# Recurrent heads of a gated linear recurrence: score outputs issued ahead of the chain of states, and a head's closing norm moved into the next head's step

## The chip, the cores and the metric

One core of one Trainium2 chip runs the whole program. The metric is the device time of one execution in microseconds (us); lower is better.

## What is computed

The program is three stacked blocks. The change touches one layer of the second, a gated linear recurrence with 16 heads of 128 key and 128 value features, run forwards and backwards over 512 tokens, each direction started from a state that 256 context tokens leave. Cut to what matters:

```python
def _chunk_gla(q, k, v, g, s0):                      # per head, chunks of tokens
    def step(state, inp):
        bcum = jnp.cumsum(gc, axis=-2)
        b_ref, b_end = bcum[..., mid:mid + 1, :], bcum[..., -1:, :]
        inter = jnp.einsum('bhck,bhkv->bhcv', qc * jnp.exp(bcum), state)
        scores = jnp.einsum('bhtk,bhsk->bhts', qc * jnp.exp(bcum - b_ref), kc * jnp.exp(b_ref - bcum))
        intra = jnp.einsum('bhts,bhsv->bhtv', jnp.where(mask, scores, 0.0), vc)
        new_state = (jnp.exp(b_end[..., 0, :])[..., None] * state
                     + jnp.einsum('bhsk,bhsv->bhkv', kc * jnp.exp(b_end - bcum), vc))
        return new_state, inter + intra

def _hgrn_readout(o, gate, norm_g, w_out):           # o = forwards + backwards
    o = _rmsnorm(o, norm_g)
    o = o.reshape(o.shape[0], o.shape[1], E_WIDTH).astype(gate.dtype)
    return (o * jax.nn.silu(gate)) @ w_out
```

## The kernel before

The function `hgrn` does the 16 heads. Its work is written out by hand as one instruction stream per engine, and `steps` calls the same `step(h, p, par, r)` on every engine: a step projects head `h` (the next one) and does the recurrence of head `p = h - 1`. Step 0 has only a projection, the last step only a recurrence, and the steps between are a loop of two steps a turn. Waits between engines are counts of marks (`PR` of TensorE, `AR` of ScalarE, `DR` of VectorE, `GM` of GpSimd).

On TensorE a step is, in this order: the projections `kf`, the context's `kf`, `kb` (`project`, line 2402: 24 matmuls each of 512 or 256 columns); the recurrence of the forward direction, `recur(p, 0)`; the projections of the context's `kb`, `g` and `q`; `recur(p, 1)` for the backward direction; and the closing sum (line 2488). `recur` has four score products `sc0` to `sc3` (line 2427), transposes of the context's and the tokens' keys (2443, 2446), the context's state (2458), the four chunks' own states (2462), and then the outputs. VectorE meanwhile masks the scores (`copy_predicated`, line 2665, marks `m0`, `m1`: `sc2` reuses the PSUM bank of `sc0` and waits for `m0`, `sc3` waits for `m1`), and makes the four states that enter the chunks one from the other (2668 and three times 2673, marks `s0`, `ch0`, `ch1`, `st`). The outputs wait for the last of them:

```python
                on(pe, DR, p, f"st{d}")
                for i in range(TT):
                    o = K.ps[:, 6, i * P:(i + 1) * P]
                    pe.matmul(o, v[:, i, :], SC[:, d, i, :], ...)
                    mm = pe.matmul(o, S[:, i, :], QI[:, i * P:(i + 1) * P], ...)
```

So of the eight products of a direction, the four of line 2468 (values times scores) and the four of line 2470 (state times queries) alternate.

After the backward direction ScalarE squares the head's output (`sq`, 2588), TensorE sums the squares over the features (`sum`, 2488), ScalarE takes logarithm and exponential (`ln`, `rstd`, 2591 and 2593), and VectorE scales and gates the output (2743, 2746). TensorE's next step starts behind the sum; `sc0` of the next head waits for `ln`, since it writes the bank of the sum.

VectorE, after the states of the backward direction, does for the next head: scans of the keys' decays (2678, 2689), `arguments` (2630 to 2638), `lower` of the weights of `kb` (2621), then the output of the head before (2743, 2746), and in the next step `other_signs` (2702, 2678, 2689), 2644, the gate (2650), `dq0` and `qi0` (`factors`, 2652, 2654), `lower` of `g` (2621) and the first mask. GpSimd's three products a direction (2612) start behind the gate.

## Time and profile before

| | us |
|---|---|
| median of 3 runs | 4802.61 (4802.16 to 4806.18) |
| the profiled execution, its own time | 4801.64 |
| its span | 4799.9 |
| first to last projection matmul of `hgrn` (line 2402) | 1869.0 to 2599.9 |
| one step of the loop, from sum to sum | 47.5 |
| TensorE, VectorE, ScalarE, GpSimd busy in it | 43.96, 33.52, 28.78, 7.10 |

A row of the timeline gives the start, the duration, the engine and line, what it writes and reads with its shape, how many instructions are merged in it, and in brackets how long the engine sat idle before and who ended that. A 128x128 product of fp32 operands shows as two matmuls. The span is 1.7 us shorter than the execution's own time, and that is 1.0 us under the median.

### The profile page before, as it was taken

How to read it: one execution, taken by the hardware profiler on the slowest of the kernel's cores; microseconds unless marked ns; L12 is line 12 of the kernel's file. 1: busy time of each engine (PE TensorE's matmuls, PEld its weight loads, DVE VectorE, ACT ScalarE, POOL GpSimd, SP SyncE). 2: the span in 40 equal slices, each digit the busy share in tenths (PEclk: the TensorE clock that was granted, in tenths of full speed). 3: DMA queues.
4: the chain of work that ended last, by engine and by line, in shares of the span. 5: the costliest groups of instructions: out<-in, count | busy, mean ns of one | idle time of the engine just before them, and what ended most of it. 6: DMA issues, size and time to landing. Idle time of an engine off the chain costs nothing. (4 is left out here: it accounts for less than half of the span.)

```text
span 4799.9 us, 79096 instructions
## 1 busy us (share of the span) xinstructions
PE 4404.9 (92%) x32172; PEld 3339.1 (70%) x32172; DVE 2461.7 (51%) x3963; ACT 1610.6 (34%) x2467; POOL 334.4 (7%) x307
## 2 busy tenths in 40 slices
PE   8898999999999989999998899978998999899987
PEld 7665787775788767888887644456877567666675
DVE  3634543433535333676766379954534355455553
ACT  2324321323322233656565210143222233333332
POOL 0120000000000000111111000000000022211220
PEclk9889999999999999999999999989998999999998
DMA  3201222221122232111110312211222210000101
GB/s 144 107 19 70 88 105 92 88 88 53 71 105 88 108 124 83 47 58 50 54 54 34 125 68 81 77 53 72 104 97 81 93 37 20 20 20 20 55 3 53
DMA packets 36638, 337.15 MB, mean 70 GB/s; under 512 B 4080, under 2 KB 6384, under 8 KB 18544
## 3 DMA queue, kind: packets, MB, share of 16 engines
q1 hardware_dynamic: 36336, 332.76, 18.7%
q8 instruction: 234, 3.83, 0.3%
q14 instruction: 68, 0.56, 0.0%
HBM read 320.16 MB, written 12.58 MB: 69 GB/s over the span
## 5 line engine op out<-in xcount | busy, mean ns | idle before, releaser
L539 PE MATMUL ps<-hi,weight_parts 128*128 128x512 f32 x5136 | 1608.6, 394 | 121.7 <-DVE lo L406 76.7
L539 PEld LDWEIGHTS ps<-hi,weight_parts 128*128 128x128 f32 x5136 | 978.1, 190 | 341.3 <-issue 123.0
L539 PE MATMUL ps<-lo,weight_parts 128*128 128x512 f32 x2568 | 1010.4, 393 | 0.0
L527 DVE TENSOR_TENSOR weight_parts<-w,weight_parts 128x1024 fp32r<-128x1024 f32 (+1 forms) x336 | 407.0, 1213 | 966.9 <-ACT weight_parts L518 966.8
L518 ACT ACTIVATE weight_parts<-w 128x1024 fp32r<-128x1024 f32 (+1 forms) x336 | 351.7, 1048 | 1199.3 <-PE ps L539 996.0
L539 PEld LDWEIGHTS ps<-lo,weight_parts 128*128 128x128 f32 x2568 | 489.4, 191 | 101.9
L3500 PEld LDWEIGHTS ps<-buffers 64*64 64x64 f32 x12544 | 431.6, 136 | 143.0 <-issue 141.3
L3500 PE MATMUL ps<-buffers 64*64 64x64 f32 x12544 | 461.2, 226 | 69.9 <-issue 43.8
L2402 PE MATMUL ps<-x_parts,column_parts 128*128 128x512 f32 x1536 | 364.9, 395 | 9.9 <-DVE column_parts L2621 9.9
L2402 PEld LDWEIGHTS ps<-x_parts,column_parts 128*128 128x128 f32 x1536 | 287.7, 189 | 75.2 <-DVE column_parts L2621 10.4
L2857 PE MATMUL ps<-x,w 128*128 128x512 f32 x768 | 332.3, 596 | 6.8 <-PEq L815 6.8
L2920 DVE SCALAR_TENSOR_TENSOR buffers<-buffers,vecs 128x392 f32<-128x392 f32 (+14 forms) x480 | 286.8, 685 | 0.0
L2857 PEld LDWEIGHTS ps<-x,w 128*128 128x128 f32 x768 | 146.8, 191 | 191.5 <-issue 191.5
L3493 PE MATMUL ps<-h,w 128*128 128x512 f32 x512 | 228.4, 600 | 1.2 <-PEq L3324 1.2
L3493 PEld LDWEIGHTS ps<-h,w 128*128 128x128 f32 x512 | 96.2, 191 | 117.1 <-issue 115.6
L2427 PE MATMUL ps<-h 128*128 128x128 f32 x1024 | 128.3, 279 | 13.4 <-DVE h L2652 13.1
L2427 PEld LDWEIGHTS ps<-h 128*128 128x128 f32 x1024 | 124.9, 196 | 17.0 <-DVE h L2652 14.2
L3756 ACT ACTIVATE buffers<-ps 128x256 f32<-128x256 f32 x160 | 61.5, 385 | 202.2 <-PE ps L3500 196.2
L2621 DVE TENSOR_TENSOR column_parts<-w,column_parts 128x1024 fp32r<-128x1024 f32 x64 | 86.2, 1349 | 80.2 <-ACT column_parts L2501 80.2
L3481 POOL TENSOR_TENSOR buffers<-buffers,const 128x512 f32<-128x512 f32 x80 | 101.6, 1270 | 290.3 <-PE ps L3500 219.8
L2601 POOL MEMSET w<- 128x1024 f32 x1 | 1.0, 951 | 1539.7 <-POOLq L2130 1539.7
L785 PE MATMUL ps<-weight_parts,hi 128*128 128x512 f32 x320 | 100.3, 395 | 0.0
(481 smaller groups left out, 5394.4 us busy)
## 6 DMA issues: line engine op xcount, KB each, us to landing
w<-in_weights SPq DMA_DIRECT2D x126, 2048.0 KB, 7.6
w<-in_wh SPq DMA_DIRECT2D x64, 512.0 KB, 3.6
v_kept<-buffers SPq DMA_DIRECT2D x4, 1024.0 KB, 5.2
buffers<-v_kept SPq DMA_DIRECT2D x16, 256.0 KB, 2.6
h<-x_kept SPq DMA_DIRECT2D x2, 2048.0 KB, 10.5
x<-in_xT SPq DMA_DIRECT2D x4, 512.0 KB, 10.8
x_kept<-h SPq DMA_DIRECT2D x1, 2048.0 KB, 7.2
vc_kept<-x SPq DMA_DIRECT2D x4, 512.0 KB, 2.6
```

The lines of the kernel that those rows point to most:

```text
L518: act.activation(K.parts[:, j % 2, 0, 0:nk, :], part_of(K, slot, j, nk, by_row), ACT.Copy)\
L527: dve.tensor_tensor(K.parts[:, j % 2, 1, 0:nk, :], part_of(K, slot, j, nk, by_row), K.parts[:, j % 2, 0, 0:nk, :].bitcast(F32), ALU.subtra ...
L539: mm = pe.matmul(ps, K.parts[:, j % 2, m, k, :], x[:, k * T:(k + 1) * T], start=(first and k == 0 and n == 0), stop=(last and k == nk - 1 ...
L785: mm = pe.matmul(K.ps[:, bank + i, :], x[:, at], w[m], start=(k == 0 and n == 0), stop=(k == 7 and n == 2), skip_group_check=True)
L2402: mm = pe.matmul(o, parts[:, half, w, k, :], src[:, m, k, 0:width], start=(k == 0 and n == 0), stop=(k == 7 and n == 2), skip_group_check= ...
L2427: mm = pe.matmul(bank[:, s], l[:, s], r[:, s], start=True, stop=True)
L2621: dve.tensor_tensor(half[:, 1], weight(name), half[:, 0].bitcast(F32), ALU.subtract).then_inc(DL.step(name), 1)
L2857: mm = pe.matmul(bank(i, j), w[:, k, j * P:(j + 1) * P], K.H[:, k, :], start=(k == 0), stop=(k == 7))
L2920: dve.scalar_tensor_tensor(y, u, w, y, ALU.mult, ALU.add).then_inc(K.sem("tapped"), 1)
L3481: pool.tensor_tensor(C, AS, on_chunks(f"{'clow' if d == 0 else 'cup'}{l}"), ALU.mult).then_inc(GM.step(f"c{l}"), 1)
L3493: mm = pe.matmul(K.ps[:, 2 + m % 2, :], w[:, k, m * P:(m + 1) * P], K.H[:, k, :], start=(k == 0), stop=(k == 7))
L3500: mm = pe.matmul(dst[hr(h)], lhsT[hr(h)], rhs[hr(h)], start=start, stop=stop, skip_group_check=True)
```

## The change

It touches only `hgrn`. In `recur` on TensorE the four products of values and scores come first and no longer wait for the states; the four products of state and queries follow in the order in which the states are made, each waiting for its own. Sum, root and output of a head leave the end of its step and become `total`, `root` and `output`, called in the next step: `total` behind the projection `kf`, `root` on ScalarE behind the forward exponentials, `output` on VectorE behind the forward `factors`. Two semaphores are new (`AN`, `DO`), and one step more on each side stands outside the loop.

```diff
--- before.py
+++ after.py
@@ -2327,25 +2327,32 @@
     AH = Marks(K, "hgrn_high", "kf kb g q")
     AZ = Marks(K, "hgrn_taken", "kf cf kb cb g q")
     AS = Marks(K, "hgrn_softplus", "ka ke kl qa qe ql qx")
-    AR = Marks(K, "hgrn_act", "rest0 kcx0 qi0 kct0 kt0 c20 c30 near1 lev1 rest1 kcx1 qi1 kct1 kt1 c21 c31 sq ln rstd")
+    AR = Marks(K, "hgrn_act", "rest0 kcx0 qi0 kct0 kt0 c20 c30 near1 lev1 rest1 kcx1 qi1 kct1 kt1 c21 c31")
+    AN = Marks(K, "hgrn_norm", "sq ln rstd")
     AD = Marks(K, "hgrn_exp", "near0 lev0")
...
     DR = Marks(K, "hgrn_dve", "kca0 dq0 qi0 m00 m10 s00 ch00 ch10 st0 "
-               "kca1 dq1 qi1 m01 m11 s01 ch01 ch11 st1 o out")
+               "kca1 dq1 qi1 m01 m11 s01 ch01 ch11 st1")
+    DO = Marks(K, "hgrn_out", "o out")
...
+    def follows(p):
+        return p is not None and not (isinstance(p, int) and p == 0)
+
     def exp_marks(d):
         return AD if d == 0 else AR
 
     def steps(eng, step):
         step(0, None, 0)
-        with eng.Fori(0, HEADS // 2 - 1) as r:
-            step(2 * r + 1, 2 * r, 1, r)
+        step(1, 0, 1, 0)
+        with eng.Fori(0, HEADS // 2 - 2) as r:
             step(2 * r + 2, 2 * r + 1, 0, r + 1)
+            step(2 * r + 3, 2 * r + 2, 1, r + 1)
+        step(HEADS - 2, HEADS - 3, 0, HEADS // 2 - 1)
         step(HEADS - 1, HEADS - 2, 1, HEADS // 2 - 1)
         step(None, HEADS - 1, 0, HEADS // 2)
 
@@ -2431,7 +2438,7 @@
...
                 if d == 0:
-                    on(pe, AR, p - 1, "ln")
+                    on(pe, AN, p - 1, "ln")
                 else:
                     on(pe, AR, p, "c20")
                 scores(p, d, 0)
@@ -2462,18 +2469,25 @@
...
-                on(pe, DR, p, f"st{d}")
                 for i in range(TT):
-                    o = K.ps[:, 6, i * P:(i + 1) * P]
-                    pe.matmul(o, v[:, i, :], SC[:, d, i, :], start=(i == 0 and d == 0), stop=False,
-                              skip_group_check=True)
-                    mm = pe.matmul(o, S[:, i, :], QI[:, i * P:(i + 1) * P], start=False, stop=(d == 1),
-                                   skip_group_check=True)
+                    pe.matmul(K.ps[:, 6, i * P:(i + 1) * P], v[:, i, :], SC[:, d, i, :], start=(i == 0 and d == 0),
+                              stop=False, skip_group_check=True)
+                for n, i in enumerate((0, 1, 2, 3) if d == 0 else (3, 2, 1, 0)):
+                    on(pe, DR, p, (f"s0{d}", f"ch0{d}", f"ch1{d}", f"st{d}")[n])
+                    mm = pe.matmul(K.ps[:, 6, i * P:(i + 1) * P], S[:, i, :], QI[:, i * P:(i + 1) * P], start=False,
+                                   stop=(d == 1), skip_group_check=True)
                 mm.then_inc(PR.step(f"o{d}"), 1)
+
+            def total(p):
+                on(pe, AN, p, "sq")
+                pe.matmul(K.ps[:, 4, :], K.c("ones"), K.sq[:, 0, :], start=True, stop=True).then_inc(PR.step("sum"), 1)
 
             def step(h, p, par, r=0):
                 if h is not None:
                     of_x(h, "kf")
+                if follows(p):
+                    total(p - 1)
+                if h is not None:
                     of_context(h, "kf")
                     of_x(h, "kb")
                 if p is not None:
@@ -2484,8 +2498,8 @@
                     of_x(h, "q")
                 if p is not None:
                     recur(p, 1, 1 - par, r - 1 + par)
-                    on(pe, AR, p, "sq")
-                    pe.matmul(K.ps[:, 4, :], K.c("ones"), K.sq[:, 0, :], start=True, stop=True).then_inc(PR.step("sum"), 1)
+                if h is None:
+                    total(p)
             steps(pe, step)
 
         @block.scalar
@@ -2506,7 +2520,9 @@
...
                 if name == "kf":
-                    on(act, DR, h - 2, "out")
+                    on(act, DR, h - 2, "kca1")
+                elif name == "g":
+                    on(act, DO, h - 2, "out")
                 act.activation(Z[par][:, dst], src, ACT.Copy).then_inc(AZ.step(name), 1)
 
             def softplus(h, par, b, cols):
@@ -2553,9 +2569,18 @@
...
+            def root(p):
+                on(act, PR, p, "sum")
+                on(act, DO, p - 1, "o")
+                act.activation(K.ln[:, :], K.ps[:, 4, :], ACT.Ln, scale=1.0 / P, bias=K.c("eps")).then_inc(AN.step("ln"), 1)
+                on(act, AN, p, "ln")
+                act.activation(K.ln[:, :], K.ln[:, :], ACT.Exp, scale=-0.5).then_inc(AN.step("rstd"), 1)
+
             def step(h, p, par, r=0):
                 if p is not None:
                     exps(p, 0, 1 - par)
+                if follows(p):
+                    root(p - 1)
                 if h is not None:
                     take(h, par, "kf")
                     take(h, par, "cf")
@@ -2585,12 +2610,9 @@
                     softplus(h, par, "q", zrest)
                 if p is not None:
                     on(act, PR, p, "o1")
-                    act.activation(K.sq[:, 0, :], K.ps[:, 6, :], ACT.Square).then_inc(AR.step("sq"), 1)
-                    on(act, PR, p, "sum")
-                    on(act, DR, p - 1, "o")
-                    act.activation(K.ln[:, :], K.ps[:, 4, :], ACT.Ln, scale=1.0 / P, bias=K.c("eps")).then_inc(AR.step("ln"), 1)
-                    on(act, AR, p, "ln")
-                    act.activation(K.ln[:, :], K.ln[:, :], ACT.Exp, scale=-0.5).then_inc(AR.step("rstd"), 1)
+                    act.activation(K.sq[:, 0, :], K.ps[:, 6, :], ACT.Square).then_inc(AN.step("sq"), 1)
+                if h is None:
+                    root(p)
             act.preload_act_table_set(LN_EXP)
             high(0, "kf")
             high(0, "kb")
@@ -2710,6 +2732,14 @@
...
+            def output(p, z):
+                on(dve, AN, p, "rstd")
+                o = OH[:, ds(p * T, T)]
+                dve.scalar_tensor_tensor(o, K.ps[:, 6, :], K.v("hgrn_norm"), K.ln[:, :], ALU.mult, ALU.mult)\
+                   .then_inc(DO.step("o"), 1)
+                on(dve, DO, p, "o")
+                dve.tensor_tensor(o, o, z[:, zg], ALU.mult).then_inc(DO.step("out"), 1)
+
             def step(h, p, par, r=0):
                 z = Z[1 - par]
                 more = h is not None and not (isinstance(h, int) and h == HEADS - 1)
@@ -2717,6 +2747,8 @@
                     other_signs(p, z)
                     context_argument(p, 0, z)
                     factors(p, 0, z)
+                if follows(p):
+                    output(p - 1, Z[par])
                 if h is not None:
                     lower(h, "g")
                 if p is not None:
@@ -2737,17 +2769,12 @@
                     arguments(h, 0, Z[par])
                 if more:
                     lower(h + 1, "kb")
-                if p is not None:
-                    on(dve, AR, p, "rstd")
-                    o = OH[:, ds(p * T, T)]
-                    dve.scalar_tensor_tensor(o, K.ps[:, 6, :], K.v("hgrn_norm"), K.ln[:, :], ALU.mult, ALU.mult)\
-                       .then_inc(DR.step("o"), 1)
-                    on(dve, DR, p, "o")
-                    dve.tensor_tensor(o, o, z[:, zg], ALU.mult).then_inc(DR.step("out"), 1)
+                if h is None:
+                    output(p, z)
             lower(0, "kf")
             lower(0, "kb")
             steps(dve, step)
-    for m in (PP, PR, AH, AZ, AS, AR, AD, DL, DS, DA, DR, GM):
+    for m in (PP, PR, AH, AZ, AS, AR, AN, AD, DL, DS, DA, DR, DO, GM):
         m.done(HEADS)
     K.done(step_pool=1, loaded=16)
 
```

How the rows of the two engines move. In TensorE's stream, end of a step's backward direction and start of the next step; `buffers` holds the values, `w` the masked scores, `h` the decayed queries, `sq` the states (as second operand) and the squares. Before:

```order
L2462 MATMUL ps<-buffers,rstd 128x128 x4
L2338 REGISTER_ALU x2
L2468 MATMUL ps<-w,buffers 128x128
L2470 MATMUL ps<-h,sq 128x128
...
L2338 REGISTER_ALU
L2488 MATMUL ps<-sq,const 128x512
L2338 ISA
L2338 REGISTER_ALU
L2402 MATMUL ps<-x_parts,column_parts 128x512 x24
L2338 REGISTER_ALU
L2402 MATMUL ps<-context_parts,column_parts 128x256 x24
```

And in the changed kernel:

```order
L2469 MATMUL ps<-buffers,rstd 128x128 x4
L2340 REGISTER_ALU
L2473 MATMUL ps<-w,buffers 128x128 x4
L2340 REGISTER_ALU
L2477 MATMUL ps<-h,sq 128x128
L2340 REGISTER_ALU
L2477 MATMUL ps<-h,sq 128x128
...
L2409 MATMUL ps<-x_parts,column_parts 128x512 x24
L2340 ISA
L2483 MATMUL ps<-sq,const 128x512
L2340 REGISTER_ALU
L2409 MATMUL ps<-context_parts,column_parts 128x256 x24
```

The sum has moved behind the first projection, and the four products of states (2477) stand apart, each with its own wait, behind the four of scores.

On VectorE, from the arguments of the next head to its first mask, before:

```order
L2621 TENSOR_TENSOR column_parts<-w,column_parts 128x1024
L2743 ISA
L2743 SCALAR_TENSOR_TENSOR buffers<-ps,vecs,ln 128x512
L2338 REGISTER_ALU
L2746 TENSOR_TENSOR buffers<-buffers,w 128x512
L2338 REGISTER_ALU
L2702 SCALAR_TENSOR_TENSOR x<-head_inputs,x 128x1536
...
L2652 TENSOR_TENSOR h<-h,head_inputs 128x512
L2338 ISA
L2654 TENSOR_TENSOR h<-h,head_inputs 128x512
L2338 REGISTER_ALU
L2621 TENSOR_TENSOR column_parts<-w,column_parts 128x1024
```

And in the changed kernel, behind the gate:

```order
L2674 TENSOR_TENSOR h<-h,head_inputs 128x512
L2340 ISA
L2676 TENSOR_TENSOR h<-h,head_inputs 128x512
L2340 ISA
L2738 ISA
L2738 SCALAR_TENSOR_TENSOR buffers<-ps,vecs,ln 128x512
L2340 ISA
L2741 TENSOR_TENSOR buffers<-buffers,w 128x512
L2340 ISA
L2643 TENSOR_TENSOR column_parts<-w,column_parts 128x1024
L2340 ISA
L2687 COPY_PREDICATED w<-const,ps 128x512
```

The two instructions of the output have moved from before `other_signs` to behind `qi0`; the number of instructions between the states of one head and the first mask of the next is the same.

## Rows read from the trace of the kernel before

**Rows 1.** Timeline of TensorE: backward end of one head, next step's forward half, next sum.

```profile
2132.17 0.49 PE L2468 MATMUL ps<-w,buffers 128*128 128x128 f32 x2 [1.30 <-DVE sq L2673]
...
2135.16 1.12 PE L2488 MATMUL ps<-sq,const 128*128 128x512 f32 x2 [0.94 <-ACT sq L2588]
2135.73 6.05 PE L2402 MATMUL ps<-x_parts,column_parts 128*128 128x512 f32 x24
...
2149.96 1.95 PE L2427 MATMUL ps<-h 128*128 128x128 f32 x16
...
2152.40 1.95 PE L2427 MATMUL ps<-h 128*128 128x128 f32 x16
...
2154.63 1.06 PE L2462 MATMUL ps<-buffers,rstd 128*128 128x128 f32 x8
2156.98 0.49 PE L2468 MATMUL ps<-w,buffers 128*128 128x128 f32 x2 [1.29 <-DVE sq L2673]
...
2158.79 3.11 PE L2402 MATMUL ps<-context_parts,column_parts 128*128 128x256 f32 x24
...
2182.66 1.12 PE L2488 MATMUL ps<-sq,const 128*128 128x512 f32 x2 [0.94 <-ACT sq L2588]
```

**Rows 2.** Timeline of VectorE over the same stretch.

```profile
2132.03 2.33 DVE L2678 TENSOR_TENSOR_SCAN x<-const,x 128x512 f32<-128x512 f32 x2
...
2140.62 0.75 DVE L2743 SCALAR_TENSOR_TENSOR buffers<-ps,vecs,ln 128x512 f32 x1
...
2142.01 1.75 DVE L2702 SCALAR_TENSOR_TENSOR x<-head_inputs,x 128x1536 f32<-128x1536 f32 x1
...
2146.19 1.22 DVE L2650 TENSOR_TENSOR head_inputs<-head_inputs,x 128x1024 f32<-128x1024 f32 x1
2147.44 0.69 DVE L2652 TENSOR_TENSOR h<-h,head_inputs 128x512 f32<-128x512 f32 x1
2148.05 1.23 DVE L2654 TENSOR_TENSOR h<-h,head_inputs 128x512 f32<-128x512 f32 x1
2149.21 1.76 DVE L2621 TENSOR_TENSOR column_parts<-w,column_parts 128x1024 fp32r<-128x1024 f32 x1
2151.17 0.74 DVE L2665 COPY_PREDICATED w<-const,ps 128x512 f32<-128x512 int32 x1 [0.20 <-PE ps L2427]
...
2155.82 1.11 DVE L2673 SCALAR_TENSOR_TENSOR sq<-sq,small,ps 128x128 f32<-128x128 f32 x3 [0.69 <-PE ps L2462]
...
2163.30 1.23 DVE L2621 TENSOR_TENSOR column_parts<-w,column_parts 128x1024 fp32r<-128x1024 f32 x1 [2.22 <-ACT column_parts L2501]
```

**Rows 3.** Busy time of each engine between the backward states and the next first mask.

```profile
2132.03:2150.96 18.93, 17.85 (x99) 15.23 (x100) 18.58 (x27) 11.71 (x16) 3.47 (x3) 1.00 0.26 76
```

**Rows 4.** Timeline of ScalarE: the root, and the last forward exponential.

```profile
2136.41 0.69 ACT L2591 ACTIVATE ln<-ps,const 128x512 f32<-128x512 f32 x1 [1.29 <-PE ps L2488]
2137.13 0.63 ACT L2593 ACTIVATE ln<-ln 128x512 f32<-128x512 f32 x1
...
2146.63 0.62 ACT L2535 ACTIVATE h<-x 128x512 f32<-128x512 f32 x1
```

**Rows 5.** Timeline of GpSimd: forward and backward products of a head.

```profile
2147.49 4.06 POOL L2612 TENSOR_TENSOR h<-h,head_inputs 128x256 f32<-128x256 f32 x3 [26.28 <-DVE head_inputs L2650]
2165.67 3.05 POOL L2612 TENSOR_TENSOR h<-h,head_inputs 128x256 f32<-128x256 f32 x3 [14.12 <-ACT h L2525]
```

**Rows 6.** Timeline of the last step: two starts of TensorE, the closing load's issue.

```profile
2621.77 3.79 PE L2427 MATMUL ps<-h 128*128 128x128 f32 x16 [10.50 <-DVE h L2652]
2636.30 1.16 PE L2427 MATMUL ps<-h 128*128 128x128 f32 x8 [2.64 <-DVE h L2652]
2647.63 0.33 SPq L2392 DMA_DIRECT2D h<-x_kept  x1
```

**Rows 7.** Granted clock (the number after the last busy time) behind the gap of 2.64 us.

```profile
2638.00:2640.00 2.00, 2.00 (x11) 2.00 (x11) 1.69 (x2) 0.27 (x1) 1.00 (x2) 0.50 0.00 0
```

More of the change, by code:

```diff
@@ L3939 @@
 args dk_exp exp_levels exp_rest softplus logsig chain
-ada_rows ada_kept ada_turned angle wave spread hgrn_pe hgrn_act hgrn_dve hgrn_pool hgrn_project hgrn_high hgrn_taken hgrn_softplus
+ada_rows ada_kept ada_turned angle wave spread hgrn_pe hgrn_act hgrn_dve hgrn_pool hgrn_project hgrn_high hgrn_taken hgrn_softplus hgrn_norm hgrn_out
 x_hi x_lo paired hgrn_exp hgrn_low hgrn_signs hgrn_args
```

## Prediction

> **What bounds it now.** I read the timeline of TensorE over one step, then VectorE's over the same stretch, since each wait of TensorE names a releaser on another engine. From sum to sum a step takes 47.50 us, 2135.16 to 2182.66 [rows 1], and all loop steps are alike to 0.05 us. TensorE stands still at three places only: 1.30 us before the outputs of each direction, released by the last of three state updates (L2673), and 0.94 us before the closing sum, released by the square [rows 1]. Everything else on it is work in a row, so TensorE sets the pace and these waits look like the gain.
>
> VectorE's rows show what comes next. From the end of the backward states (2132.03) to the end of `lower` of `g` (2150.96) it has 18.93 us with 18.58 busy in 27 instructions [rows 3], and the first mask `m0` follows at 2151.17 after an idle time of only 0.20 us [rows 2]. TensorE's `sc2` needs `m0`, and starts at 2152.40 [rows 1]: just 0.49 us after the mask's end. So between two heads VectorE is full and only half a microsecond behind being the bound.
>
> **The outputs.** The eight products take 1.81 us, 2156.98 to 2158.79 [rows 1], 0.90 for four. The chunks' own states start at 2154.63 and take four products' time too; now the score outputs follow at once (to 2156.44) and then the state outputs (to 2157.34). The updates end at 2155.82 + 1.11 = 2156.93 [rows 2], and only the last product, due to start at 2157.1, needs the last of them. So the context's `kb` starts at about 2157.3 instead of 2158.79: **1.5 us saved** in the forward direction. Four waits stand where one stood; bounds for their price are 0, as the wait for `sc1` between two groups shows no gap in 2149.96 to 2152.40, and 0.4 us (four times the 0.1 us of slack I have). I take 0: the nearest rows are such waits already granted. Behind `kb` hangs the column split on VectorE, which waits 2.22 us for ScalarE at 2163.30 [rows 2]; it moves with TensorE, and VectorE has room for that. So the 1.5 us stay, up to the backward states.
>
> **The end of a step.** The same 1.5 us, the 0.94 us wait and part of the sum go here too, and the next projection starts at about 2132.4 instead of 2135.73, 3.3 us earlier [rows 1]. The sum now stands behind `kf` and costs what it did, 0.57 us to the next matmul (2135.16 to 2135.73) and some 0.4 us of slower first matmuls, which were there before. TensorE then reaches `sc0` at 2147.2, where it was at 2149.96 [rows 1]. But the backward states, from which VectorE's full stretch counts, do not move: 2132.1. What it has to do until `m0` is the same list. The output's two instructions, 1.39 us from 2140.62 to 2142.01, leave their place before `other_signs` and stand behind `qi0` [rows 2]. So the gate ends 1.39 us earlier, at 2146.02, `dq0` at 2146.7, and `m0` starts as late as ever. This 3.3 us is therefore no gain: TensorE will wait for the mask instead.
>
> **Where `m0` lands.** From the gate's end to `m0` it is now 3.55 us (2147.41 to 2150.96), and 1.39 us more with the output. GpSimd's three products run in this stretch: 4.06 us forwards, 3.05 us backwards [rows 5], and VectorE's two instructions under the forward ones take 1.16 and 1.75 us to the next start [rows 2], where the like of the first takes 0.61 (L2652) and the like of the second 1.23 (at 2163.30): 1.1 us are lost to GpSimd. With the output in it the stretch has five instructions against the same three products. From below the output takes the blows instead of adding any, and its PSUM-reading half none: a loss of 0.5 us. From above each product of GpSimd blocks VectorE for its whole 1.0 us and an instruction more is stretched: 1.7 us. Laid out one behind the other, with the third product now blocking the output's second half and not `lower`, I get 1.2 us, 0.1 more than now. Then `m0` starts at 2146.02 + 5.03 = 2151.05, without the idle 0.20, and ends at 2151.79; `sc2` starts at 2151.84 instead of 2152.40: **0.55 us saved**. The second mask follows without a gap and is ready for `sc3`.
>
> The Trainium skill (SBUF — State Buffer, "SBUF: two separate sides") says that a VectorE instruction with two SBUF inputs and a reading GpSimd instruction exclude each other for the whole instruction, and the loser waits. The rows above agree as far as `qi0` and `lower` go. By it the first half of the output, with one input in PSUM, runs free and the second half waits, which moves nothing in the sum by more than 0.1 us; it speaks against a cheaper `m0`.
>
> **The rest.** `root` (1.35 us, 2136.41 to 2137.76) leaves the path of the sum and stands behind the last forward exponential, which ran at 2146.63 [rows 4] and now about 1.4 us earlier, at 2145.2. `ln` is then done at 2146.5 and `rstd` at 2147.1, before `sc0` (2147.2) and the output (2147.8 or later) ask for them. ScalarE's takes and `high` of `g` come 0.1 us later than before and are needed at 2151.2. The SP queue's loads wait for the outputs and come earlier by what those do. Two steps more outside the loop are code, not work: the last two steps, outside it already, run at 47.5 us as well, so 0, at most 3 us once.
>
> Sum of the engines' terms: step 1 saves 1.5 us (its `m0` has no output before it in either kernel); steps 2 to 15 save 1.5 + 0.55 = 2.05 each, 28.7; the last step gets its `dq0` 1.4 us earlier, TensorE having waited 10.50 us for it [rows 6], and its backward outputs 1.5 us earlier, and the closing load is issued right behind these (2647.63) [rows 6]: 2.9. Together 33.1 us.
>
> **The clock.** TensorE's wait for `m0` is one gap: transposes over at about 2149.8, `sc2` at 2151.84, so 2.0 us per step. Today's largest gap in a step is 1.30 us, and the granted clock is 1.00 throughout [rows 3]. In the last step a gap of 2.64 us [rows 6] was followed by a clock of 0.50 [rows 7], that is 1.2 GHz instead of 2.4. There 16 score matmuls took 3.79 us [rows 6] against 1.95 at full clock [rows 1], so a fall costs about 1.6 us, and here it would hit exactly the path from `sc2` to the outputs. Between 1.30 (never) and 2.64 (fell), 2.0 us lies in the middle: bounds are no step and all 14, 0 to 22 us. I take 5 of 14, **8 us lost**.
>
> Forecast: 4801.64 - 33.1 + 8 = 4776.5 us for a profiled execution; it lay 1.0 us under the median, so **4777 us**, 0.5% faster. A measurement can tell about 0.2%, 9.6 us.
>
> **Rivals.** (a) The clock never falls, or GpSimd costs less: 4802.6 - 33.1 = 4769.5, and with 0.5 us less lost to GpSimd in 14 steps 4762.5. For it: clock 1.00 in every step now. Chance 0.22. (b) GpSimd costs VectorE 0.6 us more per step, 8.4 us, which widens TensorE's gap to 2.6 us, and at 2.64 the clock did fall: with 9 falls, 14 us, it is 4802.6 - 33.1 + 22.8 = 4792. Chance 0.14. (c) The change does not do what it says, because each of the four granted or nearly granted waits stops TensorE and the state outputs start with the last state as before: then only the score outputs are gained, 0.9 us, and 0.55 at the mask: 14 steps of 1.45, 0.9 and 2.3 for the first and last, 23.5 in all, so 4779 without falls, 4787 with those of the forecast, and with all of them, 22 us, the same as before. Against it: no gap is seen at granted waits. Chance 0.08. (d) **Slower**: the low clock lasts from `sc2` to the forward outputs in every step. That is 2158.79 - 2152.40 less the wait of 1.30 and its latencies, about 4.9 us of TensorE work [rows 1], which doubles: +4.9 - 2.05 = +2.85 a step, 14 steps +40, less 4.4 of the first and last: 4838. It decides where more than 3.05 us of work a step run at the low clock (33.1 + 9.6 over 14). Against it: it needs a fall in every step, behind a gap shorter than any that is seen to bring one here. Chance 0.04.
>
> **Numbers.** The forecast has 0.52. Its own range, 2 to 9 falls and 0.2 us of mask time either way, is 4769 to 4786. The range of all cases reaches from (a) to (b), 4763 to 4793, leaving out (d), the slow end of (c) and what is beyond (b). Faster by more than 0.2%: the forecast, (a), most of (b) and (c), 0.87; within: 0.09; slower: 0.04.
>
> **What would show it.** In the changed profile: state products (L2477) without a wait over 0.2 us before the first three; kb's context projection 2.7 us behind the start of L2469; no wait before the sum; a new wait of TensorE of 2 us for VectorE's first mask (L2687), with VectorE busy without a gap from the backward states to it; steps of 45.4 us, some of them 47 where the granted clock is below 1. It would be wrong if the steps shrank by 4 us or more (then VectorE's stretch was not the bound), if `sc0` waited for `ln`, or if VectorE waited for `rstd` before the output.

## The result, and the profile after

The changed kernel takes 4750.59 us (median of 4, 4747.28 to 4753.98) against 4802.39 us (4798.81 to 4806.18) for the kernel before on the same chip: a ratio of 0.9893, interval 0.9878 to 0.9907, or 51.8 us less. That is faster, as forecast, but by twice the 25 us that were forecast, and below the range (4763 to 4793). Its profiled execution took 4748.9 us, with a span of 4746.7.

Laid beside each other, the two traces give the difference in three pieces. The stage of the heads, from its first projection to the issue of its closing load, shrank from 778.6 us (1869.01 to 2647.63 [rows 6]) to 740.0 (1871.6 to 2611.60): 38.6 us. It starts 2.6 us later. The recurrence of the last mixer, a layer over a thousand microseconds later whose code the change does not touch, takes 809.8 us where it took 828.6: 18.8 us, both from its first small product to the same matmul near its end (3859.54 to 4688.14 in before; to its very last small product it is 835.7 and 818.0). All other work is 2 us longer. 38.6 - 2.6 + 18.8 - 2.1 is the 52.7 us between the two profiled executions.

**The heads.** TensorE's timeline of the changed kernel, from one moved sum to the next:

```profile
2129.90 1.02 PE L2483 MATMUL ps<-sq,const 128*128 128x512 f32 x2
2130.36 3.44 PE L2409 MATMUL ps<-context_parts,column_parts 128*128 128x256 f32 x24
...
2139.10 1.95 PE L2434 MATMUL ps<-h 128*128 128x128 f32 x16
...
2143.11 2.05 PE L2434 MATMUL ps<-h 128*128 128x128 f32 x16 [1.41 <-DVE w L2687]
...
2145.45 1.06 PE L2469 MATMUL ps<-buffers,rstd 128*128 128x128 f32 x8
2146.34 1.06 PE L2473 MATMUL ps<-w,buffers 128*128 128x128 f32 x8
2147.24 1.06 PE L2477 MATMUL ps<-h,sq 128*128 128x128 f32 x8
2148.05 3.12 PE L2409 MATMUL ps<-context_parts,column_parts 128*128 128x256 f32 x24
...
2174.76 1.02 PE L2483 MATMUL ps<-sq,const 128*128 128x512 f32 x2
```

The waits of 1.30, 1.29 and 0.94 us [rows 1] are gone: own states, score products and state products stand without a gap, and so does the sum. One wait is new in the loop, 1.41 us before `sc2`, for the first mask; the list of TensorE's waits (total, times, longest) has it 14 times, with a longest of 1.8 us:

```profile
PE ps L2434 <- DVE w L2687: 22.3, 14, 1.8
```

Sum to sum is 44.86 us here and 45.53 in the step before. The loop does two steps a turn, and the mean of the two is 45.19, against 47.50. The windows of these two steps show the granted clock, the number after the five engines, at 1.00:

```profile
2084.37:2129.90 45.53, 43.68 (x279) 38.96 (x278) 33.63 (x55) 28.71 (x43) 6.13 (x6) 1.00 0.18 55
2129.90:2174.76 44.86, 43.45 (x279) 38.89 (x278) 32.95 (x53) 28.62 (x42) 6.13 (x6) 1.00 0.18 56
```

VectorE's timeline over the stretch that [rows 2] show of before, and GpSimd's row there:

```profile
2123.59 2.33 DVE L2700 TENSOR_TENSOR_SCAN x<-const,x 128x512 f32<-128x512 f32 x2
...
2136.36 1.22 DVE L2672 TENSOR_TENSOR head_inputs<-head_inputs,x 128x1024 f32<-128x1024 f32 x1
2137.61 0.69 DVE L2674 TENSOR_TENSOR h<-h,head_inputs 128x512 f32<-128x512 f32 x1
2138.22 1.24 DVE L2676 TENSOR_TENSOR h<-h,head_inputs 128x512 f32<-128x512 f32 x1
2139.38 0.74 DVE L2738 SCALAR_TENSOR_TENSOR buffers<-ps,vecs,ln 128x512 f32 x1
2140.16 1.14 DVE L2741 TENSOR_TENSOR buffers<-buffers,w 128x512 f32 x1
2141.21 1.21 DVE L2643 TENSOR_TENSOR column_parts<-w,column_parts 128x1024 fp32r<-128x1024 f32 x1
2142.35 0.71 DVE L2687 COPY_PREDICATED w<-const,ps 128x512 f32<-128x512 int32 x1
```

```profile
2137.66 3.08 POOL L2634 TENSOR_TENSOR h<-h,head_inputs 128x256 f32<-128x256 f32 x3 [24.88 <-DVE head_inputs L2672]
```

The moved output stands between `qi0` and `lower`, and VectorE has no idle time up to the mask. The stretch from the gate's end (2136.36 + 1.22) to `m0` is 4.77 us. GpSimd's three forward products take 3.08 us where they took 4.06 [rows 5]. `lower` is back at 1.21 us from 1.76 [rows 2]; only `qi0` and the second half of the output are stretched beside GpSimd.

Behind the loop it is not so. In the last step the sum waits 2.50 us for the square, and the granted clock is 0.50 from there through the forward scores, which wait for VectorE in both kernels; the gap before the backward scores is 4.17 us where it was 2.64 [rows 6].

**The last mixer.** Its 12,544 small products, on the page of before and of the changed kernel (count, busy time, mean ns of one, idle time before them, and what ended most of it):

```profile
L3500 PE MATMUL ps<-buffers 64*64 64x64 f32 x12544 | 461.2, 226 | 69.9 <-issue 43.8
```

```profile
L3527 PE MATMUL ps<-buffers 64*64 64x64 f32 x12544 | 460.0, 226 | 52.0 <-issue 27.1
```

The work is the same to 1.2 us; the idle time before it fell by 17.9 us. The part of it that the profile puts down to "issue" (the engine waited for nothing that the profile shows) fell by 16.7. The timeline of one stretch of it, in before and then in the changed kernel, both ending at the same `L3569`/`L3596` matmul (4037.79 and 4003.29):

```profile
4023.78 0.46 PE L3500 MATMUL ps<-buffers 64*64 64x64 f32 x5 [1.22 <-issue]
...
4028.57 0.68 PE L3500 MATMUL ps<-buffers 64*64 64x64 f32 x16 [0.95 <-issue]
...
4033.29 0.97 PE L3500 MATMUL ps<-buffers 64*64 64x64 f32 x27 [1.01 <-issue]
```

```profile
3988.11 2.08 PE L3527 MATMUL ps<-buffers 64*64 64x64 f32 x64 [0.60 <-issue]
...
3996.28 2.72 PE L3527 MATMUL ps<-buffers 64*64 64x64 f32 x85 [0.27 <-issue]
...
4000.49 1.96 PE L3527 MATMUL ps<-buffers 64*64 64x64 f32 x60 [0.44 <-issue]
```

Three stalls of 3.18 us together became three of 1.31, and they stand elsewhere in the code. Over the whole recurrence before has 47 gaps of more than 0.6 us, 58.8 us in all, and the changed kernel 27, 36.3 us in all.

### The profile page after: what moved, and what is told of

It reads as the page before. It is cut to its first block and busy times, and to the rows that moved or that the text cites. A ratio compares the mean times of both kernels' runs of the same rounds, so it can differ in the third digit from the quotient of the medians.

```text
span 4746.7 us, 79005 instructions
## 1 busy us (share of the span) xinstructions
PE 4400.7 (93%) x32172; PEld 3338.7 (70%) x32172; DVE 2457.6 (52%) x3963; ACT 1608.9 (34%) x2467; POOL 320.5 (7%) x307
## 5 line engine op out<-in xcount | busy, mean ns | idle before, releaser
L3527 PE MATMUL ps<-buffers 64*64 64x64 f32 x12544 | 460.0, 226 | 52.0 <-issue 27.1
L2434 PE MATMUL ps<-h 128*128 128x128 f32 x1024 | 129.4, 281 | 35.0 <-DVE w L2687 22.3
L2409 PE MATMUL ps<-context_parts,column_parts 128*128 128x256 f32 x768 | 104.0, 292 | 0.0
```

What stands on the lines that cost most here:

```text
L2409: mm = pe.matmul(o, parts[:, half, w, k, :], src[:, m, k, 0:width], start=(k == 0 and n == 0), stop=(k == 7 and n == 2), skip_group_check= ...
L2434: mm = pe.matmul(bank[:, s], l[:, s], r[:, s], start=True, stop=True)
L3527: mm = pe.matmul(dst[hr(h)], lhsT[hr(h)], rhs[hr(h)], start=start, stop=stop, skip_group_check=True)
```

## The experiments

"Heads" is the time from the first projection of `hgrn` to the first score of its last step (752.8 us before, 717.1 changed), "mixer" the last mixer between the two matmuls named above (828.6 and 809.8), both from the profiled execution.

### The written-out steps alone

`unroll_only`: the kernel before with the changed `steps`.

```diff
         step(0, None, 0)
-        with eng.Fori(0, HEADS // 2 - 1) as r:
-            step(2 * r + 1, 2 * r, 1, r)
+        step(1, 0, 1, 0)
+        with eng.Fori(0, HEADS // 2 - 2) as r:
             step(2 * r + 2, 2 * r + 1, 0, r + 1)
+            step(2 * r + 3, 2 * r + 2, 1, r + 1)
+        step(HEADS - 2, HEADS - 3, 0, HEADS // 2 - 1)
```

> The kernel before, with only the changed kernel's steps function (steps 1 and 14 written out beside the loop). The heads' stage should stay as it was, 778.6 us from its first projection to the closing load. Theory A (where the later code lies sets how long the 64-column matmuls of the last mixer take, through gaps that the profile calls issue): the mixer's stage is about 17 us shorter, total 4780 to 4790 us. Theory B (the 17 us belong to the changed work of the heads or are chance of the runs): total 4798 to 4806 us.

Measured: 4786.8 us against 4803.84, ratio 0.9967 (0.9958 to 0.9977). Heads 752.5, unchanged; mixer 811.3. So nearly all that the last mixer gained (17.3 of the 18.8 us) comes from the form of the loop alone: an edit that moves no work anywhere is worth 17 us, in another layer.

### Each part alone

`outputs_only`: before, with the reordered products of `recur`.

```diff
-                on(pe, DR, p, f"st{d}")
...
+                for n, i in enumerate((0, 1, 2, 3) if d == 0 else (3, 2, 1, 0)):
+                    on(pe, DR, p, (f"s0{d}", f"ch0{d}", f"ch1{d}", f"st{d}")[n])
```

> The kernel before, with only the eight output products reordered (values times scores first, states as they are made). My theory of the heads' stage: 1.5 us per step from the forward outputs and nothing from the backward ones, since the square waits for ScalarE's softplus: the stage is 24 us shorter, a step takes 46.0 us. Rival (the backward ones count too): 44.5 to 45.5 us a step, 35 to 48 us. Theory A: the code hardly moves, so the last mixer keeps its time within 5 us, total 4774 to 4783; theory B says the same of it, but if the mixer follows the earlier arrival, total 4762 to 4768.

`norm_only`: the changed kernel, with the old order of the products and the one wait ahead of them.

```diff
+                on(pe, DR, p, f"st{d}")
...
-                for n, i in enumerate((0, 1, 2, 3) if d == 0 else (3, 2, 1, 0)):
-                    on(pe, DR, p, (f"s0{d}", f"ch0{d}", f"ch1{d}", f"st{d}")[n])
```

> The changed kernel with the old order of the eight output products: only sum, root and output moved. Heads' stage: 0.5 to 0.8 us a step (46.8 us a step), some 9 to 13 us in all, since VectorE sets the first mask. Theory A: 17 us more from the last mixer, as the steps are written out as in the changed kernel: total 4771 to 4777. Theory B: total 4788 to 4794. If instead the wait before the sum was on the path, 2.7 us a step and 43 us from the stage alone.

Measured: `outputs_only` 4794.11, ratio 0.9984 (0.9975 to 0.9994); heads only 4.1 us shorter, where 24 were expected for the stage. `norm_only` 4777.32, ratio 0.9952 (0.9935 to 0.9968); heads 11.8 us shorter, steps of 46.80, and its mixer has the 17 us of the written-out steps too. In the heads, 4.1 and 11.8 are far from the 35.7 of both together. The timeline of `outputs_only` around the end of a step shows why:

```profile
2133.46 1.68 PE L2488 MATMUL ps<-sq,const 128*128 128x512 f32 x2 [2.50 <-ACT sq L2588]
2134.16 6.16 PE L2402 MATMUL ps<-x_parts,column_parts 128*128 128x512 f32 x18
```

and its window behind the sum:

```profile
2134.00:2137.00 3.00, 3.00 (x7) 1.99 (x6) 3.00 (x8) 1.71 (x3) 0.00 (x0) 0.50 0.46 158
```

The backward outputs are done 1.5 us earlier, but the square is not ready any earlier, so the wait before the sum grows from 0.94 to 2.50 us, and behind it the granted clock is 0.50, that is 1.2 GHz instead of 2.4. Twelve of 14 steps are 47.5 us long, the two without a fall 45.92. A fall costs the whole gain, 1.63 us. The wait before the sum is 2.50 to 2.54 us in all these steps, in the two without a fall as well.

`outputs_filled` tests that: eight products of constants stand in the gap. Their result is overwritten by the sum, so nothing is left out.

```diff
                     recur(p, 1, 1 - par, r - 1 + par)
+                    for _ in range(8):
+                        pe.matmul(K.ps[:, 4, 0:P], K.c("ones"), K.c("ones"), start=True, stop=True)
```

> The kernel with only the output products reordered, and in TensorE's 2.5 us gap before the sum eight matmuls of 128 columns whose result is overwritten. Theory of the clock: with the gap filled the granted clock stays at 1.00 in every step, steps take 45.95 us instead of 47.55 in 12 of 15, and the total falls by 16 to 22 us against the outputs-only kernel, to 4772 to 4778. Rival (the low clock is chance, or costs nothing because the path runs elsewhere): total 4792 to 4797.

Measured: 4778.5 us, ratio 0.995 (0.9933 to 0.9967). Heads 729.2 us, 19.4 less than in `outputs_only`, and 12 falls of 1.63 us are 19.6. The gap left is under a microsecond:

```profile
2126.38 1.95 PE L2488 MATMUL ps<-const 128*128 128x128 f32 x16
2129.05 1.12 PE L2490 MATMUL ps<-sq,const 128*128 128x512 f32 x2 [0.72 <-ACT sq L2590]
```

All steps take 45.91 to 45.97 us, and the granted clock is 1.00 in every one. Filling an idle engine with useless work made the kernel 15.6 us faster than `outputs_only`. The account now closes: the outputs' 4.1 us, plus 12 falls of 1.63, plus the norm's 11.8 are 35.5 us of the 35.7. The two parts do not multiply each other; the moved sum removes the gap in which the first part loses its gain.

### Why the last mixer became faster

`pad_before`: before, with 128 increments of a semaphore that nobody waits for (`apart`) on TensorE's queue ahead of the heads. `pad_64` and `pad_256` have 64 and 256.

```diff
+            for _ in range(128):
+                K.apart(pe)
             steps(pe, step)
```

> The kernel before, with 128 semaphore increments, which nobody waits for, on TensorE's queue at the start of the heads' stage, where it waits 9.9 us for the first weights anyway. Theory A: heads' stage as before (778.6 us and at most 3 us for the increments), but the last mixer 3 us or more away from its time, up or down. Theory B: nothing moves beyond 3 us.

> The kernel before with 64 increments. Stalls moved by 64 records; the increments' 13 us stand beside the wait of 9.9 us for the first weights, 3 to 5 us lost. Mixer between 810 and 830 us by theory A, which gives no number for a given shift; total that plus the rest, 4790 to 4810. Rival (only whether there is padding counts): 815.5 us again.

> The kernel before with 256 increments instead of 128 on TensorE at the start of the heads' stage. The stalls of the last mixer stood 256 TensorE records apart and moved by exactly 128 of them with 128 increments. If they are ends of blocks of 256 instructions, a shift by 256 is none: stalls at the same places as in the kernel before, mixer 826 to 832 us (815.5 with 128), heads' stage as before, its start 42 to 46 us later, total 4843 to 4850. Rival (later code, or later arrival, helps by itself): mixer 816 us or less, total 4830 to 4836.

`unroll_tensor` writes the steps out on TensorE's queue alone, `unroll_others` on ScalarE's, VectorE's and GpSimd's but not TensorE's (`written_out` is the changed kernel's `steps`):

```diff
-            steps(pe, step)
+            written_out(pe, step)
```

```diff
-            steps(act, step)
+            written_out(act, step)
...
-            steps(pool, step)
+            written_out(pool, step)
...
-            steps(dve, step)
+            written_out(dve, step)
```

> The kernel before, with the two steps written out beside the loop on TensorE alone. If the place of TensorE's own later code sets the last mixer's time: mixer about 811 us between the same two matmuls instead of 828.6, total 4783 to 4790. If the other engines' code does: mixer 828 us, total 4800 to 4806.

> The kernel before, with the two steps written out on ScalarE, VectorE and GpSimd and not on TensorE. If TensorE's own code place is what counts: mixer 828 us, total 4800 to 4806. If the others' does: mixer 811, total 4783 to 4790. If both do, each gives a part.

Measured, each against before on its own chip (p: the place of the first group of stalls in the records of TensorE's two queues, weight loads, matmuls and the sequencer's records together, modulo 256; where the count starts is arbitrary, so only differences of p say something):

| | median | ratio (interval) | mixer | p |
|---|---|---|---|---|
| before | | | 828.6 | 9 |
| `unroll_others` | 4803.54 | 1.0000 (0.9990 to 1.0009) | 832.7 | 9 |
| `unroll_tensor` | 4789.04 | 0.9970 (0.9958 to 0.9981) | 814.3 | 148 |
| `pad_64` | 4798.54 | 0.9991 (0.9982 to 1.0001) | 816.0 | 201 |
| `pad_before` | 4809.95 | 1.0014 (1.0004 to 1.0023) | 815.5 | 137 |
| `pad_256` | 4842.10 | 1.0082 (1.0065 to 1.0099) | 829.7 | 9 |

The pads pay for themselves at the start of the heads (TensorE's first projection comes behind 16.2, 26.2 and 45.8 us without a matmul there instead of 9.9; the increments stand 0.15 us apart), so their medians say little; the mixer is what they are for. Three things follow. It is TensorE's own code that matters, since the others' left the mixer no shorter. Within each of four stretches of the mixer the stalls stand whole multiples of 256 records apart, to one or two records, and a pad of N moves them back by N modulo 256: 9 to 201, to 137, and with 256 to 9 again. (Three waits of 3.4 to 4.3 us and one of 0.8 that the profile also calls issue are not of this kind: they stay at the same matmuls in every kernel.) And 256 gives the mixer its old time back. The 816.0 us of `pad_64` would fit its rival too; it is the places, and `pad_256`, that speak against it. At one and the same place the mixer's time still differs by 3 to 4 us from run to run: 828.6, 829.7 and 832.7 at p = 9, and 814.3 and 811.3 (`unroll_only`) at 148. The timeline of `pad_256` has the very stalls of before, at the same matmuls:

```profile
4062.04 0.46 PE L3502 MATMUL ps<-buffers 64*64 64x64 f32 x5 [1.22 <-issue]
...
4067.37 0.68 PE L3502 MATMUL ps<-buffers 64*64 64x64 f32 x16 [1.49 <-issue]
...
4072.09 0.97 PE L3502 MATMUL ps<-buffers 64*64 64x64 f32 x27 [1.01 <-issue]
```

The page's rows of the same products, of `pad_64` and of `pad_256`:

```profile
L3502 PE MATMUL ps<-buffers 64*64 64x64 f32 x12544 | 460.4, 226 | 51.5 <-issue 24.2
```

```profile
L3502 PE MATMUL ps<-buffers 64*64 64x64 f32 x12544 | 461.5, 225 | 68.1 <-issue 42.1
```

The queue that brings instructions moved this much in before and in the changed kernel:

```profile
q8 instruction: 234, 3.83, 0.3%
```

```profile
q8 instruction: 238, 3.90, 0.3%
```

Every packet of this queue has 16,384 bytes in the trace. The Trainium skill (Perfetto Trace Analysis, "The 4-stage abstract model") says that an instruction has 64 bytes; by that figure, an estimate, 256 of them would be one such packet.

The trace also ties packets to stalls. In before, the DMA view of 4021.0 to 4022.4 us holds one packet, and that of 4022.4 to 4026.2 none:

```profile
q8 instruction: 1, 0.02, 5.0%
```

```profile
DMA packets 0, 0.00 MB, mean 0 GB/s; under 512 B 0, under 2 KB 0, under 8 KB 0
```

That packet ended at 4022.35, the next two at 4027.29 and 4031.95, and the three stalls shown for before end at 4023.78, 4028.57 and 4033.29: 1.43, 1.28 and 1.34 us behind them. So it is with all 42 such stalls over 0.25 us in that mixer, 1.2 to 1.6 us behind the end of a packet, and with 574 of 603 in the 15 traces; of times taken every half microsecond only some 6% lie so. That TensorE stalls at the end of a block of 256 instructions until the next block has come is therefore supported by places, sizes and times alike. The 42 stalls are 42.4 us in before, the 37 of the changed kernel 26.0. Not settled is how much a given place is worth, that is at which of its block ends TensorE arrives too early. At p = 144 and 148 the mixer gained 14 to 19 us, at 201 and 137 some 13, in three kernels of the next section, at 131 to 140, 4 to 9, and at 129 (`outputs_filled`, 827.6) and 118 next to nothing or a loss.

### Where the new wait can go

The changed kernel still waits 1.41 us a step for `m0`. `late_output` puts the output behind the masks, ahead of the first state copy; TensorE waits for its first half (which reads the bank of the outputs) before the score products.

```diff
+                if d == 0 and follows(p):
+                    on(pe, DO, p - 1, "o")
...
-                if follows(p):
-                    output(p - 1, Z[par])
...
-                    recur(p, 0)
+                    recur(p, 0, (lambda: output(p - 1, Z[par])) if follows(p) else None)
```

> The changed kernel, with VectorE's two output instructions moved on, from before the first mask to between the two masks and the copy of the entering state, where it waits 1.70 us, and a wait of TensorE for them before the products of values and scores. If VectorE's full stretch up to the first mask bounds the step (my theory), TensorE's 1.41 us gap before the third scores closes and a step takes 43.8 to 44.0 us instead of 45.2: 18 to 20 us less than the changed kernel, total 4730 to 4734. Rival: GpSimd's third product or another wait (lev2, ln) holds the third scores: within 5 us of the changed kernel, 4746 to 4752.

Measured: 4751.36, ratio 0.9897 (0.9881 to 0.9914), no better than the change and 17 us above the expected total. The heads gained 8.3 us (steps of 44.60 in the mean), 0.6 us a step, and the mixer (819.4, p = 138) gave back 9.6. TensorE's wait did not vanish, and VectorE's timeline tells what was late next, ScalarE's `high` of `g`, on which `lower` waits:

```profile
2137.91 2.05 PE L2434 MATMUL ps<-h 128*128 128x128 f32 x16 [0.81 <-DVE w L2689]
```

```profile
2135.78 1.44 DVE L2645 TENSOR_TENSOR column_parts<-w,column_parts 128x1024 fp32r<-128x1024 f32 x1 [0.93 <-ACT column_parts L2517]
2137.14 0.71 DVE L2689 COPY_PREDICATED w<-const,ps 128x512 f32<-128x512 int32 x1
```

**Second step.** `late_split` adds to that: `lower` of `g` goes behind the masks and the whole of `recur(p, 0)` on VectorE, and 7 increments on TensorE are meant to place the code. `late_placed` is the same with 20. `late_folded` has none, and TensorE's wait for the output is folded into the one for the first state copy, which VectorE does after it.

```diff
+                if p is not None:
+                    recur(p, 0, (lambda: output(p - 1, Z[par])) if follows(p) else None)
                 if h is not None:
                     lower(h, "g")
-                    recur(p, 0, (lambda: output(p - 1, Z[par])) if follows(p) else None)
...
+            for _ in range(7):
+                K.apart(pe)
```

> The kernel with the late output, and the column split of g (L2645, which waited 0.93 us for ScalarE ahead of the first mask) moved behind the forward states, and 7 increments on TensorE, which put the stalls of the last mixer near where the kernels with 810 us have them. If VectorE's list up to the first mask was what bounds, TensorE's gap before the third scores (0.81 us) closes, a step takes 43.7 to 43.9 us instead of 44.6, the heads' stage is 11 to 13 us shorter than with the late output; mixer 810 to 814 us: total 4730 to 4736, faster than both kernels. Rival: g comes too late for its projection or delays the backward arguments, and steps stay at 44.6 us: total 4742 to 4746.

> The kernel with late output and late column split of g, with 20 increments on TensorE instead of 7. This shifts the stalls of the last mixer by 13 records, to where the changed kernel has them. If their place alone sets the mixer's time: mixer 808 to 813 us as in the changed kernel, heads' stage as with 7, total 4719 to 4725. Rival (the mixer's time follows something else, such as when it is reached): 821 us again, total 4731 to 4736.

```diff
-                if d == 0 and follows(p):
-                    on(pe, DO, p - 1, "o")
+                if d == 0:
+                    on(pe, DR, p, "s00")
...
-                    on(pe, DR, p, (f"s0{d}", f"ch0{d}", f"ch1{d}", f"st{d}")[n])
+                    if d or n:
+                        on(pe, DR, p, (f"s0{d}", f"ch0{d}", f"ch1{d}", f"st{d}")[n])
```

> The heads as with the late column split, but without increments, and with TensorE's wait for the output folded into the wait for the entering state, which VectorE copies behind it. The kernel with 20 increments moved the last mixer's stalls away from those of the changed kernel instead of to them (a sign of mine) and its mixer took 830 us. Here TensorE has as many instructions as in the changed kernel, so its stalls should stand where that kernel's do. If their place sets the mixer's time: mixer 808 to 813 us, steps 43.35 us, total 4719 to 4725. Rival (any of the late kernels has a mixer of 820 us and more, for another reason): total 4730 to 4742.

| | median | ratio (interval) | heads | mixer | p |
|---|---|---|---|---|---|
| changed | 4750.59 | 0.9893 (0.9878 to 0.9907) | 717.1 | 809.8 | 144 |
| `late_split` | 4733.32 | 0.9855 (0.9838 to 0.9871) | 690.95 | 821.5 | 131 |
| `late_placed` | 4742.08 | 0.9864 (0.9848 to 0.9881) | 691.1 | 830.4 | 118 |
| `late_folded` | 4736.71 | 0.9842 (0.9826 to 0.9859) | 691.0 | 824.6 | 140 |

Steps are 43.35 us in the mean, 1.84 less than in the changed kernel. In all three kernels TensorE has no gap over 0.15 us in any step of the loop: its own work is the bound again. In `late_folded` the scores run without a gap and VectorE waits for TensorE, not TensorE for it:

```profile
2130.89 1.95 PE L2434 MATMUL ps<-h 128*128 128x128 f32 x16
...
2133.33 1.95 PE L2434 MATMUL ps<-h 128*128 128x128 f32 x16
```

```profile
2132.10 0.75 DVE L2690 COPY_PREDICATED w<-const,ps 128x512 f32<-128x512 int32 x1 [0.85 <-PE ps L2434]
```

`late_folded` beats both kernels: 1.58% below before, its interval apart from the changed kernel's. (Before took 4804.44 us beside `late_split`, 4809.54 beside `late_placed` and 4812.31 beside `late_folded`, so only the ratios compare. Those of the three overlap, so which of them is fastest is not shown.) The total of `late_split` fell into its range by two misses that cancel: its heads were 17.9 us shorter than those of `late_output`, where 11 to 13 were expected, and its mixer took 821.5 us instead of 810 to 814. Placing the mixer's code did not work. The 20 increments were counted in the wrong direction and moved the stalls from 131 to 118, where the mixer took 9 us more, on another chip. `late_folded` put them at 140 instead of 144, and its mixer missed the expected 808 to 813 by 12 us or more. Its page shows that most of this is stalls again: 36.5 us of issue where the changed kernel has 27.1, and 3.3 us more of busy time.

```profile
L3531 PE MATMUL ps<-buffers 64*64 64x64 f32 x12544 | 463.3, 226 | 61.6 <-issue 36.5
```

Whether four records of place, the other chip or the earlier arrival brought them stays open.

## Why the prediction was right and wrong

**Right:** the bound. VectorE between the backward states and the first mask sets the pace, and the earlier end of a step became a wait for `m0` (22.3 us over 14 waits). When `late_split` and `late_folded` took the output and `lower` out of that stretch, the steps shrank by 1.84 us more. With the 0.70 us of `norm_only` that is 2.5 of the 3.3 us at a step's end that were held there. No wait came before `sc0`, the output or the state products.

**The outputs**, forecast 1.5 us: from 47.50 to 45.92 where the clock held, 1.58, and with the norm in place 46.80 to 45.19, 1.61. The granted waits cost nothing. **The mask**, forecast 0.55: `norm_only` gives 0.70. From the gate to `m0` I had 5.03 us and it is 4.77, because the output took GpSimd's blows in place of `lower` and `dq0` to `qi0` lost no more. The rule cited in the prediction (the Trainium skill, SBUF — State Buffer, "SBUF: two separate sides") holds in these rows: the half with an operand in PSUM took 0.74 us beside GpSimd, the half with two in SBUF 1.14, and 0.69 in `late_output`, where no GpSimd product runs beside it. GpSimd's three products took 1 us less than beside two-operand work alone.

**The sum of the heads**, forecast 33.1: 38.6. Of the 5.5 missing, 3.6 are the two terms above over 14 steps (2.31 each instead of 2.05), and the rest is in the first and last step, 6.3 instead of 4.4. In the last step TensorE's wait for `dq0` is 8.49 us where it was 10.50 [rows 6]:

```profile
2588.69 3.78 PE L2434 MATMUL ps<-h 128*128 128x128 f32 x16 [8.49 <-DVE h L2674]
```

**The clock**, forecast 8 us lost: nothing in the loop. I placed a gap of 2.0 us halfway between 1.30 and 2.64; it was 1.4 to 1.8, and the clock stayed at 1.00 in every step of the loop. Counted from the end of the backward states (2123.59 in the changed kernel, 2132.03 before), `m0` started 0.26 us earlier than laid out (18.76 for 19.02), and `sc0` 0.34 us later (15.51 for 15.17). The mechanism itself is real, at 2.50 us, in `outputs_only`. There it takes all that the first part brings, so the parts had to be costed together, which I did without noticing: "nothing from the backward outputs" holds in time, but their gap is what the moved sum removes.

**The step that failed** is "Two steps more outside the loop are code, not work": costed at 0, at most 3 us once, it brought 17 to 19 us in the last mixer. I argued it from the written-out steps' own speed, in the heads, where it is indeed 0 (752.5 against 752.8). I did not look at what lies behind: 43.8 us of idle time put down to "issue" stood in the group of the page with the most instructions. Unexplained idle time five times my term for the clock was left aside. What the runs showed in its place: the two steps, written out on TensorE's queue alone, move the block ends of all its later code, and with them the stalls (`unroll_tensor` 14.3 us, `unroll_only` 17.3; on the other engines' queues alone, nothing gained).

The misses add up: 18.8 us of the mixer, 8 of the clock and 5.5 of the heads, less 4.7 for the later start and the other work, are the 27.6 us between the forecast of 4776.5 and the profiled 4748.9. Without the mixer's 18.8 us the kernel would have taken some 4769 us, which is what rival (a), no fall of the clock, was worked out to give (4769.5), and just inside the range; the mixer took it out. That agreement is partly luck: the heads gave 5.5 us more than in rival (a), and the 4.7 us took nearly all of it back.

## What to carry to other kernels

Cost a new gap on TensorE together with the clock behind it: shortening work ahead of a wait can bring nothing until the wait is filled or gone, and the wait should be filled or removed in the same edit. When a wait moves to another engine's full stretch, look for an instruction in that stretch that nobody asks for soon, and put it behind the one that is asked for: here that was worth more a step than the mask's whole term. And when TensorE shows idle time for "issue" in dense code of small matmuls, any change of its code ahead of there, even in another layer, can move the total, here by up to some 20 us; before crediting an edit, compare the stages that it doesn't touch.

## What the runs showed of the hardware

- TensorE stalls of 0.3 to 1.8 us in dense 64x64 products, whole multiples of 256 of its records apart within a stretch; the last mixer takes 810 to 833 us with identical work as they shift.
- Each of the 42 such stalls in the mixer of before ends 1.2 to 1.6 us behind the end of a 16,384-byte packet of the queue that brings instructions.
- Behind gaps of 2.50 us in every step the granted clock fell to 0.50 in 12 of 14 steps, at 1.63 us each. Behind the changed kernel's gaps of 1.4 to 1.8 us it did not fall.
- Increments of a semaphore on TensorE's queue stood 0.15 us apart: 128 of them made a wait of 26.2 us, 256 one of 45.8.
- The same kernel had medians of 4802.39 to 4812.31 us on different chips, as much as 0.2%: only ratios to before on the same chip compare.
